# Two more joined slots in the expert stage: 96 tokens of a small expert beside 32 tokens of a wide one

## The reference

```python
logits = einsum('td,de->te', xt, w_router) + b_router
top_val, top_idx = top_k(logits, 4)                 # 4 of 32 experts for each token
gates = softmax(top_val)
# for each expert e, over the tokens xb that chose it:
hb = xb @ w1[e] + b1[e]                             # 1024 -> 2048
x_glu, x_lin = min(hb[:, :1024], 7), clip(hb[:, 1024:], -7, 7)
act = x_glu * sigmoid(1.702 * x_glu) * (x_lin + 1)
y  += gate * (act @ w2[e] + b2[e])                  # 1024 -> 1024
```

## Time and profile before

| | |
|---|---|
| median of three runs | 2528.4 us |
| the profiled execution's own time | 2529.57 us |
| its span in the trace | 2527.8 us |
| expert stage, TensorE's first to last instruction | 883.7 to 2505.8 us |
| TensorE busy | 2373.7 us, 94% |
| share of the chain that ended last | TensorE 63% |
| mean granted TensorE clock | 0.973 |
| HBM read | 469.39 MB |

### The profile page before, as it was taken

How to read it: one execution, slowest core, us unless ns; L and a number is a source line. 1 busy time by engine, 2 the same in 40 slices (tenths; PEclk the granted TensorE clock), 3 DMA queues, 4 the chain that set the end, 5 groups by cost and what they waited for, 6 DMA issues and landing times.

```text
span 2527.8 us, 29031 instructions
## 1 busy us (share of the span) xinstructions
PE 2373.7 (94%) x11228; PEld 1560.8 (62%) x11229; DVE 627.6 (25%) x1535; ACT 362.1 (14%) x817; POOL 431.2 (17%) x1003
## 2 busy tenths in 40 slices
PE   7899987989987599999999999999999999999996
PEld 4446555534443285869596785866858758758442
DVE  2131156223243721112121221212212212212112
ACT  3002045112221000001101011010110110111012
POOL 3705883011001000000001000010010000000002
PEclk9999988999999799999999999999999999999998
DMA  8604110710003647986878878788788888888974
GB/s 201 144 23 50 57 21 2 216 67 1 0 1 152 224 152 274 368 256 221 255 249 269 275 254 271 261 273 278 257 260 273 275 285 288 289 284 296 312 250 156
DMA packets 373631, 508.09 MB, mean 201 GB/s; under 512 B 49257, under 2 KB 234921, under 8 KB 373492
## 3 DMA queue, kind: packets, MB, share of 16 engines
q1 hardware_dynamic: 361416, 470.03, 56.3%
q0 software_dynamic: 10896, 35.88, 6.1%
q10 hardware_dynamic: 1180, 0.30, 0.1%
HBM read 469.39 MB, written 38.25 MB: 201 GB/s over the span
## 4 chain that ended last, share of the span: by engine, by line
PE 63%; ACT 1%; DVE 0%; POOL 0%; issue 0%; DMA 0%; ACTq 0%; POOLq 0%
PE ps L2111 28%; PE ps L2184 20%; PE ps L2198 10%; PE ps L2078 1%; PE ps L2088 1%; PE ps L2124 1%; PE ps L2141 1%; ACT xT L2460 1%; PE ps L2165 1%; ACT actT L2507 0%; POOL rs L293 0%; DMA xg<-xn_dram,gx 0%; DVE outT L2270 0%; DVE tail L2394 0%; DVE tail L2396 0%
## 5 line engine op out<-in xcount | busy, mean ns | idle before, releaser
L2184 PE MATMUL ps<-xT,we 128*128 128x160 f32 (+9 forms) x3584 | 516.5, 307 | 1.4 <-ACT xT L2460 1.4
L2184 PEld LDWEIGHTS ps<-xT,we 128*128 128x128 f32 x3584 | 508.1, 190 | 15.4 <-issue 8.3
L2111 PE MATMUL ps<-we,xT 128*128 128x512 f32 (+1 forms) x1152 | 479.0, 594 | 0.0
L2111 PEld LDWEIGHTS ps<-we,xT 128*128 128x128 f32 (+1 forms) x1152 | 198.8, 184 | 246.6 <-issue 246.6
L2198 PE MATMUL ps<-actT,we 128*128 128x160 f32 (+9 forms) x1792 | 261.1, 307 | 0.0
L2198 PEld LDWEIGHTS ps<-actT,we 128*128 128x128 f32 x1792 | 253.4, 190 | 5.6 <-DVE outT L2348 2.0
L2111 PE MATMUL ps<-we,actT 128*128 128x512 f32 (+1 forms) x576 | 240.9, 596 | 0.7 <-ACT actT L2507 0.7
L2483 ACT ACTIVATE sg<-glu 128x512 f32<-128x512 f32 (+9 forms) x90 | 48.5, 539 | 1006.7 <-DVE glu L2303 515.8
L1989 POOL DMA_INDIRECT acc_dram<-orow,sx x43 | 66.5, 1546 | 693.6 <-ACT orow L2471 488.7
L2111 PEld LDWEIGHTS ps<-we,actT 128*128 128x128 f32 (+1 forms) x576 | 99.1, 184 | 129.1 <-issue 128.2
L801 PE MATMUL ps<-xnT,wa 128*128 128x512 f32 x384 | 169.1, 601 | 8.2 <-DMA wa<-in_w_in 8.2
(11 more groups left out here) (358 smaller groups left out, 2141.2 us busy)
## 6 DMA issues: line engine op xcount, KB each, us to landing
we<-in_w SPq DMA_DIRECT2D x384, 1024.0 KB, 6.7
wa<-in_w_in SPq DMA_DIRECT2D x4, 2048.0 KB, 13.1
xrow<-in_x SPq DMA_DIRECT2D x32, 128.0 KB, 6.8
wa<-in_w_xkv SPq DMA_DIRECT2D x2, 2048.0 KB, 9.9
h<-in_x SPq DMA_DIRECT2D x4, 1024.0 KB, 18.5
acc_dram<-h SPq DMA_DIRECT2D x1, 4096.0 KB
fin<-acc_dram SPq DMA_DIRECT2D x8, 512.0 KB, 5.8
out<-fin SPq DMA_DIRECT2D x32, 128.0 KB, 2.2
```

The lines of the kernel that those rows point to most:

```text
L2111: last = nc.tensor.matmul(m.ps[cols, bank, :], moved[:, 4 * half + k, cols], view[:, k, :], start=False, stop=(half == 1 and k == 3), skip ...
L2184: last = nc.tensor.matmul(bank[:, part * WIN:part * WIN + W], view[:, k, (j % 2) * P:(j % 2 + 1) * P], m.xT[:, k, 0:W], start=(k == 0), st ...
```

## The change

The room of ranks 27, 28 and 29 goes from 128 to 96 tokens. The slots `(28,)` and `(27,)` become `(28, 7)` and `(27, 8)`: 96 tokens of the small expert stand in columns 0 to 95, and tokens 128 to 159 of rank 7 or 8 in columns 96 to 127. The slots `(7,)` and `(8,)` themselves become narrow ones of 128 tokens. So there are 12 wide slots and 19 narrow ones, three of these joined, and the weights of ranks 7 and 8 are loaded twice: 34 times 12 pieces in place of 32 times 12. Rank 29 keeps a slot of its own.

The order changes too: `(1,)` and `(2,)` follow each other, so do `(3,)` and `(4,)`, and ten narrow slots stand at the end.

In `rows_by_weights` a part of 96 columns is issued as a matmul of columns 0 to 63 and one of columns 64 to 95, so that each chunk has three matmuls. A second `sel96` and a second half of `high` are made for the new split, with eleven more small DMAs at the stage's start, and two more instructions of VectorE. `fin`, the tile of the last stage, moves from 64 KB to 16 KB, since the ring's last pieces stand elsewhere.

```diff
@@ -46,9 +46,11 @@
-RANK_WIDTH = (256, 224, 200, 168, 164, 164, 160, 160, 160, 156, 144, 136, 136, 132) + (P,) * 16 + (64, 64)
-SLOTS = ((0,), (30, 31)) + tuple((r,) for i in range(1, 14) for r in (i, 30 - i)) + ((16,), (15,), (14,))
-SLOT_WIDTH = tuple(RANK_WIDTH[r[0]] if len(r) == 1 else P for r in SLOTS)
+RANK_WIDTH = (256, 224, 200, 168, 164, 164, 160, 160, 160, 156, 144, 136, 136, 132) + (P,) * 13 + (96, 96, 96, 64, 64)
+SPLIT = {(30, 31): (64, 0), (28, 7): (96, 1), (27, 8): (96, 1)}
+SLOTS = ((0,), (30, 31), (1,), (2,), (28, 7), (3,), (4,), (27, 8), (5,), (29,), (6,), (26,), (9,), (25,), (10,), (24,), (11,), (23,), (12,), (22,),
+         (13,), (21,), (20,), (19,), (18,), (17,), (16,), (15,), (8,), (7,), (14,))
+SLOT_WIDTH = tuple(P if len(r) == 2 or r[0] in (7, 8) else max(P, RANK_WIDTH[r[0]]) for r in SLOTS)
@@ -248,9 +250,10 @@
-    at("high", 168, [P, WIN])
+    at("high", 167, [P, 2, WIN])
-    at("low", 169.5, [P, 2])
+    at("sel96", 166, [P, P])
+    at("low", 169.5, [P, 4])
@@ -270,7 +273,7 @@
-    at("fin", 64, [P, NB, D])
+    at("fin", 16, [P, NB, D])
...
@@ -1859,12 +1862,13 @@
             if s == 0:
-                sp.dma_start(m.high[ST:P], m.gate_l[0:ST]).then_inc(high_in, 16)
-                for r in range(4):
-                    sp.dma_start(m.sel[32 * r:32 * r + 1, 0:ST], m.ones[0:1, 0:ST]).then_inc(high_in, 16)
-                    sp.dma_start(m.sel[32 * r + 2:32 * r + 3, ST:P], m.ones[0:1, ST:P]).then_inc(high_in, 16)
-                for r in (2, 3):
-                    sp.dma_start(m.sel[32 * r + 1:32 * r + 2, :], m.ones[0:1, :]).then_inc(high_in, 16)
+                for n, (sel, cut) in enumerate(((m.sel, 64), (m.sel96, 96))):
+                    sp.dma_start(m.high[cut:P, n], m.gate_l[0:P - cut]).then_inc(high_in, 16)
+                    for r in range(4):
+                        sp.dma_start(sel[32 * r:32 * r + 1, 0:cut], m.ones[0:1, 0:cut]).then_inc(high_in, 16)
+                        sp.dma_start(sel[32 * r + 2:32 * r + 3, cut:P], m.ones[0:1, cut:P]).then_inc(high_in, 16)
+                    for r in (2, 3):
+                        sp.dma_start(sel[32 * r + 1:32 * r + 2, :], m.ones[0:1, :]).then_inc(high_in, 16)
@@ -1941,13 +1945,14 @@
             if paired[s]:
-                pool.wait_ge(high_in, 16 * 11)
-                for i, x in enumerate(experts):
-                    g.tensor_copy(m.gx[:, c, i:i + 1], m.idx_g[:, bass.ds(x * NB, 1)]).then_inc(idx_ok if i else low_ok, 1)
-                    g.tensor_copy(m.sx[:, c, i:i + 1], m.idx_s[:, bass.ds(x * NB, 1)]).then_inc(idx_ok if i else low_ok, 1)
-                g.tensor_tensor(m.low[:, 1:2], m.gate_l[:, bass.ds(e * NB, 1)], m.low[:, 0:1], ALU.mult).then_inc(low_ok, 1)
+                pool.wait_ge(high_in, 16 * 22)
+                n, tile = (64, 96).index(SPLIT[SLOTS[s]][0]), SPLIT[SLOTS[s]][1]
+                for i, x in enumerate((e * NB, experts[1] * NB + tile)):
+                    g.tensor_copy(m.gx[:, c, i:i + 1], m.idx_g[:, bass.ds(x, 1)]).then_inc(idx_ok if i else low_ok, 1)
+                    g.tensor_copy(m.sx[:, c, i:i + 1], m.idx_s[:, bass.ds(x, 1)]).then_inc(idx_ok if i else low_ok, 1)
+                g.tensor_tensor(m.low[:, 2:3], m.gate_l[:, bass.ds(e * NB, 1)], m.low[:, n:n + 1], ALU.mult).then_inc(low_ok, 1)
-                g.tensor_tensor(m.gs[:, c, 0:1], m.low[:, 1:2], m.high[:, bass.ds(experts[1] * NB, 1)], ALU.add).then_inc(idx_ok, 1)
+                g.tensor_tensor(m.gs[:, c, 0:1], m.low[:, 2:3], m.high[:, n, bass.ds(experts[1] * NB + tile, 1)], ALU.add).then_inc(idx_ok, 1)
@@ -1963,8 +1968,9 @@
                 if paired[s]:
-                    for i in range(2):
-                        pool.indirect_dma_start(xg[q % 2][ST * i:ST * i + ST, :], None, a.xn_dram, bass.IndirectOffsetOnAxis(m.gx[0:ST, s % 3, i:i + 1], 0),
+                    first = SPLIT[SLOTS[s]][0]
+                    for i, (lo, hi) in enumerate(((0, first), (first, P))):
+                        pool.indirect_dma_start(xg[q % 2][lo:hi, :], None, a.xn_dram, bass.IndirectOffsetOnAxis(m.gx[0:hi - lo, s % 3, i:i + 1], 0),
                                                 bounds_check=last_token, oob_is_err=False).then_inc(gathered[q % 2] if i else pair_in, 16)
...
@@ -2098,6 +2105,12 @@
+        def row_sel(s):
+
+            if not paired[s]:
+                return m.ones
+            return m.sel if SPLIT[SLOTS[s]][0] == 64 else m.sel96
+
@@ -2105,11 +2118,14 @@
             for x in range(shared):
                 piece_ready(s, shared * i + x)
                 views.append(piece_view(m, s, shared * i + x))
+            columns = [[slice(0, P)]]
+            if shared == 2:
+                columns = [[slice(0, 64)], [slice(64, P)]] if SPLIT[SLOTS[s]][0] == 64 else [[slice(0, 64), slice(64, 96)], [slice(96, P)]]
             for k in range(4):
-                for x, view in enumerate(views):
-                    cols = slice(ST * x, ST * x + ST) if shared == 2 else slice(0, P)
-                    last = nc.tensor.matmul(m.ps[cols, bank, :], moved[:, 4 * half + k, cols], view[:, k, :], start=False,
-                                            stop=(half == 1 and k == 3), skip_group_check=True)
+                for view, parts in zip(views, columns):
+                    for cols in parts:
+                        last = nc.tensor.matmul(m.ps[cols, bank, :], moved[:, 4 * half + k, cols], view[:, k, :], start=False,
+                                                stop=(half == 1 and k == 3), skip_group_check=True)
             return last
 
         def narrow(s):
...
@@ -2269,8 +2285,10 @@
         v.memset(m.outT[:], 0.0).then_inc(init_f, 1)
         v.memset(m.sel[:], 0.0).then_inc(init_f, 1)
+        v.memset(m.sel96[:], 0.0).then_inc(init_f, 1)
         v.memset(m.high[:], 0.0).then_inc(init_f, 1)
-        v.tensor_scalar(m.low[:, 0:1], m.at_row[:, 0:1], float(ST), None, ALU.is_lt).then_inc(init_f, 1)
+        v.tensor_scalar(m.low[:, 0:1], m.at_row[:, 0:1], 64.0, None, ALU.is_lt).then_inc(init_f, 1)
+        v.tensor_scalar(m.low[:, 1:2], m.at_row[:, 0:1], 96.0, None, ALU.is_lt).then_inc(init_f, 1)
         v.memset(m.xg1[:], 0.0).then_inc(init_f, 1)
         v.memset(m.brow[:], 1.0).then_inc(init_f, 1)
```

More of the change, by code:

```diff
@@ L1846, in _ @@
         regs = [sp.alloc_register(f"expert_sp{i}") for i in range(4)]
-        sp.wait_ge(init_f, 8)
+        sp.wait_ge(init_f, 10)
         for s in range(NS):
@@ L1982, in scatter @@
                 if paired[s]:
-                    pool.indirect_dma_start(a.acc_dram, bass.IndirectOffsetOnAxis(m.sx[0:ST, s % 3, 0:1], 0), orow[q % 2][0:ST, :], None,
+                    first = SPLIT[SLOTS[s]][0]
+                    pool.indirect_dma_start(a.acc_dram, bass.IndirectOffsetOnAxis(m.sx[0:first, s % 3, 0:1], 0), orow[q % 2][0:first, :], None,
                                             bounds_check=last_row, oob_is_err=True, compute_op=ALU.add).then_inc(pair_out, 16)
                     pool.wait_ge(pair_out, 16 * paired[:s + 1].count(True))
-                    pool.indirect_dma_start(a.acc_dram, bass.IndirectOffsetOnAxis(m.sx[0:ST, s % 3, 1:2], 0), orow[q % 2][ST:P, :], None,
+                    pool.indirect_dma_start(a.acc_dram, bass.IndirectOffsetOnAxis(m.sx[0:P - first, s % 3, 1:2], 0), orow[q % 2][first:P, :], None,
                                             bounds_check=last_row, oob_is_err=True, compute_op=ALU.add).then_inc(scattered[q % 2], 16)
@@ L1990, in scatter @@
                                         bounds_check=last_row, oob_is_err=True, compute_op=ALU.add).then_inc(scattered[q % 2], 16)
-        pool.wait_ge(init_f, 8)
+        pool.wait_ge(init_f, 10)
         columns(0)
@@ L2120, in narrow @@
             if paired[s]:
-                pe.wait_ge(high_in, 16 * 11)
+                pe.wait_ge(high_in, 16 * 22)
             for r in range(4):
                 k = 3 if paired[s] else 2 if r >= 2 else 1
-                last = nc.tensor.matmul(m.ps[:, r, :], (m.sel if paired[s] else m.ones)[32 * r:32 * r + k, :], m.brow[32 * r:32 * r + k, s % 2, :],
+                last = nc.tensor.matmul(m.ps[:, r, :], row_sel(s)[32 * r:32 * r + k, :], m.brow[32 * r:32 * r + k, s % 2, :],
                                         start=True, stop=False, skip_group_check=True)
@@ L2140, in narrow @@
                 k = 3 if paired[s] else 1
-                last = nc.tensor.matmul(m.ps[:, 4 + n, :], (m.sel if paired[s] else m.ones)[32 * n:32 * n + k, :], m.crow[32 * n:32 * n + k, s % 2, :],
+                last = nc.tensor.matmul(m.ps[:, 4 + n, :], row_sel(s)[32 * n:32 * n + k, :], m.crow[32 * n:32 * n + k, s % 2, :],
                                         start=True, stop=False, skip_group_check=True)
@@ L2212, in broad @@
                 second(j, range(KC))
-        pe.wait_ge(init_f, 8)
+        pe.wait_ge(init_f, 10)
         x_in(0)
```

## The result

The changed kernel takes 2620.35 us (median of five runs, 2614.85 to 2621.41), against 2527.12 for the kernel before (five runs). The ratio, estimated from all the runs and so not quite the quotient of the two medians (1.0369), is 1.0362, with a 95% interval of 1.035 to 1.0373. The profiled execution took 2621.36 us, with a span of 2619.6; the forecast for a profiled execution was 2622.0 and for the median 2621.

What follows compares the result with a forecast made beforehand. TensorE's instruction stream in the expert stage was taken as the bound. Exchanged slots, -15.9 us, and mixed-width chunks, +108.3, gave +92.4: 2622.0 us profiled, 2621 median (own range 2612 to 2636, wide range 2575 to 2660).

Steps and rivals of the forecast that it cites:

- What bounds the kernel: Expert stage: TensorE's instruction stream in program order sets the time, if the weights still come in time.
- Two wide slots for two narrow ones: Expert stage: two wide slots go, 108.4 us less; two plain narrow slots come, 89.2 us more.
- Turning the rows between two wide slots: Wide slot before a wide one: the third block waits for VectorE's copy, 4.35 us each; all turning 0.3 more.
- The start of the stage: Expert stage's start: VectorE's extra memset, double-size memset and tiny operation add 0.6 us, between 0.2 and 1.
- The joined slots and the change of shape: Two new joined slots: +2.4 us for joining, +108.3 for two shape changes and separate streaming in each of 96 chunks.
- The weights: Expert stage: 24 more 1 MB pieces cost 0 us of waiting, 3 as upper bound.
- Side by side: Joined slots' chunks: all three parts run at once, a chunk stays 0.858 us; 2512.5 us in all; chance 0.15.
- One after another without cost: Joined slots' chunks: 4 passes, 1.716 us, shape changes free; +66.5 us, 2595 in all; chance 0.06.
- All three in a row: Joined slots' chunks: even the two 32s run one after another; +174.8 us, 2703 in all; chance 0.03.
- The rule: Joined slots: by the skill's rule, going between 128x64 and 128x32 drains TensorE, so the change is slower.

Runs made afterwards that it cites:

- the last run: Changed kernel with 96 columns as three matmuls of 32, the order of before and one more joined slot (29, 6): 2497.44 us, ratio 0.9878 to the kernel before.
- grouped: Changed kernel with the 64-column matmuls of all four chunks issued ahead of the 32-column ones: 2595.01 us, ratio 1.0279 to the kernel before.
- quarters: Changed kernel with the 96 columns issued as three matmuls of 32, not one of 64 and one of 32: 2513.5 us, ratio 0.9946 to the kernel before.

## Why the prediction was right, step by step

- **What bounds the kernel**: TensorE's stream in the expert stage. The stage grew by 91.2 us and the span by 91.8; 92.4 were forecast for the whole.
- **Two wide slots for two narrow ones**, -108.4 + 89.2. The narrow slot is 45.95 us after as before. Confirmed by one more such exchange, expected at 9.8 us and measured at 9.7.
- **Turning the rows between two wide slots**, 4.35 us each. 4.73 and 4.34: right, 0.4 too little in all. Not forecast were the lower clock behind one of them, 20.10 - 18.52 = 1.6 us (18.52 in the trace before, above), and a wait of 0.35 us for VectorE's outputs in slot (4,). The clock had cost the profile before 1.6 us in its first slot, and these two cancel.
- **The start of the stage**, +0.6. It is there: VectorE's work from its first memset to its copy of the biases, behind which GpSimd begins, took 876.53 - 871.20 = 5.33 us before and 877.21 - 871.41 = 5.80 after, and TensorE's wait for the first gathered rows grew from 17.41 to 17.89. Right, 0.1 too much.
- **The joined slots and the change of shape**, +2.4 and +108.3, in all 110.7. Measured: (102.8 - 48.4) x 2 = 108.7. The 2 us too many are counted twice: the 1.2 of a joined slot already holds entering and leaving the shape once for each row, 12 times 0.15, and so do the chunks. A chunk itself was forecast at 1.986 us and took 1.985. That a shape of 32 columns costs 0.12 a visit was worked out from the other two; the windows give 1173.13 - 1172.15 - 0.858 = 0.12, and 1172.15 - 1171.15 - 0.858 = 0.14 for 64.
- **The weights**, 0 us: no wait, even where the joined slots take 50 us. The prediction reads a DMA share of 0.91 as 9% short of the limit; that reading is wrong, since the trace before has 1.09 at 386 GB/s just ahead of the stage, and the last run 1.07 at 372 GB/s from 1650 to 1700 us, in the stage. There was more room than it allowed for.
- **What is luck.** 92.4 against 91.8 is closer than the single terms are: 2.0 us too many for the joined slots stand against 0.4 too few for turning the rows, 0.35 for the wait in slot (4,), and some 0.1 a slot where a slot's length differs from the sum of its parts; and the two falls of the clock happen to be equal.
- **The rivals.** Side by side: 32 columns never start while 64 stream, and this is what decided. One after another without cost: the grouped form shows the cost of the changes by itself, 19.4 us for 72 pairs of changes fewer, 0.27 a pair. All three in a row: the 32s run in pairs (x2 in the windows).
- **The rule.** By the rule of the Trainium skill, "TensorEngine Tiling (Array Packing)", section "Key Properties", a change of mode, not of the tile, drains TensorE. What the earlier trace rows left open is shown: 128x64 to 128x32 is such a change, at 0.27 us for there and back, and what hurts more is that nothing of one mode runs beside the other. (The list of modes that the prediction quotes stands in the same page's section "Available Configurations".)

The forecast was weighed too low: the case side by side, at 0.15, had not much for it, since in the earlier trace rows a change of the column count alone already cost as much as any other. The range's upper end, 2660, wasn't needed.

## What to carry to other kernels

Small matmuls share TensorE's array only if they have one shape: 64 + 32 + 32 columns cost two streams and two changes of shape (1.985 us a chunk), 32 + 32 + 32 + 32 cost one stream (7.00 / 8 = 0.88). When parts of different width are to stand beside each other, cut all of them to the smallest width: here, with float32 and 512 streamed columns, four matmuls of 32 took no longer than two of 64. Other types and shorter streams were not tried. And the price of a change that the trace doesn't show can stand in another stage: here the attention's rows gave the expert stage's cost to within 2 us of 108.

## What the runs showed of the hardware that was not expected

- Behind a wait of 2.40 us the granted clock was 0.66 over 5 us; behind one of 2.79 us, in the same kernel and the same kind of slot, the second layer shows no fall (24.27 us for it, 24.36 in the timeline before). It is so in all three profiles with this order: behind the same wait of 2.40 us quarters has 0.68 and grouped 0.66 over 5 us, and neither falls behind 2.79. Why the shorter wait is the one that costs stays open.
- Four parts of 32 columns in a chunk, each with weights and stream of its own, take 7.00 us in eight chunks, 0.02 less than two parts of 64. In the chunks of the changed kernel the first pass of 32 columns takes 0.45 us and that of 64 columns 0.48, which would account for it.
- The DMA share of a profile can be over 1: 1.09 at 386 GB/s just ahead of the stage. Slots of 50 us that use 24 pieces each had 0.99 and 1.00, at 349 and 355 GB/s, and TensorE didn't wait for a piece once.
